# A hybrid trunk step on one core: first loads in order of need, and the first projection chunk with its parts outermost

## The chip, the cores and the metric

The kernel runs on one core of a Trainium2 chip. The metric is the device time of one execution in microseconds (us). The engines are TensorE (PE), VectorE (DVE), ScalarE (ACT) and GpSimd (POOL); SyncE (SP) only issues DMAs here.

## What is computed

One layer of a hybrid diffusion trunk over 384 tokens: 128 context tokens and 256 latent ones. The part that the change touches is its beginning:

```python
ada = silu(c) @ w_ada + b_ada                       # (1024) @ (1024, 6 * 1024), for context and for latents
sh1, sc1, g1, sh2, sc2, g2 = split(ada, 6)
n = rmsnorm(h, norm1_g) * (1 + sc1) + sh1           # h: 384 tokens x 1024
z = n @ w_in                                        # split into 14 parts: v, ic, q, k, u, ...
```

Behind it come neighbourhood attention, a gated convolution, a two-way gated scan (HGRN2), their mix through w_out, and a mixture of 64 experts with a shared one. All is fp32.

## The kernel before

All engines walk one list, `SCHEDULE`, built by `schedule()` (L161). A stage of it is issued by each engine that has a part in it, in the list's order, and semaphores join them; each engine works strictly in that order. An event `("unit", n)` is one group of products with one PSUM bank, `n % 2`. PE makes unit n only when unit n - 2 has been copied out by ACT.

Units 0 to 3 are adaLN: silu(c) times a piece of 512 columns of w_ada (L1534), eight products of 32 x 512 each, so that four pieces give shift and scale of the first norm. The units behind them are projections. The chunks "v" and "ic" are 512 columns of w_in each, with tokens on the partitions: three units of eight products (over k, the eight parts of D = 1024) by way of `product` (L1504). An fp32 product leaves two records in the trace, so a unit has 16.

Weights come through a ring of three slots of 2 MB in bigA. SP issues the loads in the order of `STREAM`: four pieces of w_ada, then "v", "ic", "q", "k" and so on. The load number n waits until the slot's earlier owner, n - 3, has been used. So w_ada's fourth piece waits for the first unit. x (1.5 MB) and the constants K (1.1 MB: identity, masks and so on) stand behind the third and fourth load in SP's order, and the two caches of 256 KB go on ACT's queue. POOL waits for the constants and then loads and masks attention's bias tiles.

The stage "norm1" stands after unit 1: ACT squares the three token tiles (L670), DVE makes the inverse root and the scaled tiles XN (L1088). The stage "mod1" stands after unit 3. PE first turns the 2048 modulation values into columns by 16 products with two moving columns (L1584, 32 records); each reads every eighth column of ADA. Then it transposes XN part by part (L1592), 24 transposes into banks 2 to 5. DVE forms the columns (L1056 to L1059) and writes the modulated nT from PSUM, two instructions for each part k (L1043, L1046). The first unit of "v" starts when all eight parts are written:

```python
if c == 0:
    pe.wait_ge(n_ready, KD)
```

Behind "v" ACT copies its units to V and rounds nT for the split products of "q" and the others; "ic" follows on PE directly. The split chunks, attention, the scan, the gates and the experts follow in the same list.

Of the kernel before, what the change touches and what calls it, by code (L numbers as in the profile page):

```python
# [21 lines left out]
P = 128  # L22
D = 1024
KD = D // P
NT = 3
# [27 lines left out]
K_ID, K_MASK, K_LEV, K_SCAN, K_SEL, K_TRI, K_ONE, K_R128, K_TOK, K_COL, K_T8, K_END, K_SUB = range(13)  # L53
K_W = [P, GRID_W, 7 * P, T, 2 * P, P, P, P, NT * 4, 2, NG * NG, 0, RTAB]
# [7 lines left out]
def shape_constants():  # L62
# [33 lines left out]
STREAM = ([("ada", n) for n in range(4)]  # L96
          + [x for n, name in enumerate(IN_CHUNKS)
             for x in [("in", n)] + ([("ada", ADA_IN[name])] if name in ADA_IN else [])]
# [14 lines left out]
def projection_units():  # L113

    units = []
    for n in range(4):
        units.append(("ada", n, 0))
# [96 lines left out]
def trunk(nc, x, consts, cols, b_gate, w_ada, w_in, w_br, w_out, rpb, cache_k, cache_v, state, w_router, b_router,  # L214
# [4 lines left out]
    with ExitStack() as ctx:  # L219
# [45 lines left out]
        ADA = bigB[:, 6144:8192]  # L265
        pair = sel[:, :, 0]
# [115 lines left out]
        xnt_ready = sem("normed_transposed")  # L382
        n_ready = sem("modulated")
# [3 lines left out]
        csil_zero = sem("csilu_padding_zeroed")  # L387
# [33 lines left out]
        at_zero = sem("pairwise_terms_zeroed")  # L421
# [76 lines left out]
        y_back = [sem(f"parts_loaded_{m}") for m in range(4 * NT)]  # L498
# [10 lines left out]
        def slot(key):  # L509
            return ring[:, SLOT_OF[key] % NSLOT, :]  # L510

# [31 lines left out]
        def _(sp):  # L543
# [106 lines left out]
        def _(act):  # L650
# [7 lines left out]
            act.dma_start(CK, cache_k).then_inc(in_cache, 16)  # L658
            act.dma_start(CV, cache_v).then_inc(in_cache, 16)
            for ev in SCHEDULE:  # L660
                st = ev[0]
                if st == "csilu":
                    act.wait_ge(in_cols, 16)
                    act.wait_ge(csil_zero, 1)
# [1285 lines left out]
```

## Time and profile before

| what | us |
|---|---|
| median of three runs | 1268.3 |
| lowest and highest run | 1262.52, 1287.38 |
| profiled execution, its time | 1289.7 |
| profiled execution, its span | 1287.9 |
| PE busy in it | 1162.2 |
| DVE, ACT, POOL busy in it | 446.9, 287.9, 180.8 |

The span runs from the first to the last instruction of one profiled execution. The profile page gives totals; the rows further down come from queries of the same trace: timelines by engine, lists of waits, DMA issues, and sums over stretches of time. In a timeline the first number is the start, the second the length, and the bracket holds the idle time ahead and what ended it. The granted clock is that of PE as a share of its full speed; the two levels are 1.2 and 2.4 GHz.

### The profile page before, as it was taken

Reading aid. Unit: us, or ns where it says so; the run is one execution under the profiler, and the core shown is the slowest. Engines: PE = TensorE matmul, PEld = TensorE weight load, DVE = VectorE, ACT = ScalarE, POOL = GpSimd, SP = SyncE. Lnnn points to the kernel's source line nnn. Section 1 sums busy time; section 2 is a strip of 40 time slices with the busy share of each in tenths; the row PEclk is TensorE's granted clock in tenths of the full one; section 3 lists DMA queues with packets and bytes.
Section 4 is the critical chain, followed back from the end, with each engine's and each line's share of the span. In section 5 each row is a group of like instructions: output and inputs, shape, how many; then the busy total and the mean of one; then the engine's idle time right before and its main releaser. Section 6 shows DMA issues by size and latency. Waiting matters only on the chain.

```text
span 1287.9 us, 14753 instructions
## 1 busy us (share of the span) xinstructions
PE 1162.2 (90%) x4912; PEld 713.0 (55%) x4912; DVE 446.9 (35%) x945; ACT 287.9 (22%) x429; POOL 180.8 (14%) x163
## 2 busy tenths in 40 slices
PE   2899988899988887799987999999999999999965
PEld 0549877678777765556454444444444444444422
DVE  0313333442787964333353121121221212212116
ACT  1022433334533432300121111111111111111101
POOL 0200222100332300000000411111111111111100
PEclk9799988889989998798987989999999999999978
DMA  9813555437444332140033869999999999999464
GB/s 355 219 65 131 95 81 79 74 132 274 160 151 153 125 139 82 53 142 17 1 131 157 319 259 386 401 390 377 378 393 387 376 386 407 392 392 391 178 275 181
DMA packets 85971, 292.40 MB, mean 227 GB/s; under 512 B 10330, under 2 KB 14554, under 8 KB 70682
## 3 DMA queue, kind: packets, MB, share of 16 engines
q1 hardware_dynamic: 69408, 259.10, 52.0%
q0 software_dynamic: 12976, 27.29, 9.2%
q10 hardware_dynamic: 3540, 5.39, 1.3%
q8 instruction: 29, 0.48, 0.2%
q14 instruction: 18, 0.15, 0.0%
HBM read 284.79 MB, written 25.30 MB: 241 GB/s over the span
## 4 chain that ended last, share of the span: by engine, by line
PE 55%; DVE 5%; DMA 2%; ACT 1%; issue 1%; DVEq 0%; SPq 0%; POOLq 0%
PE PS L1829 15%; PE PS L1504 12%; PE PS L1846 7%; PE PS L1831 7%; PE PS L1848 4%; PE PS L1815 3%; PE PS L1514 2%; PE PS L1896 1%; DMA bigA<-in_w_sh_down 1%; PE PS L1864 1%; PE PS L1695 1%; PE PS L1702 0%; DMA bigA<-y_parts 0%; PE PS L1676 0%; DVE bigC L1482 0%
## 5 line engine op out<-in xcount | busy, mean ns | idle before, releaser
L1552 PE MATMUL PS<-bigB_r 128*128 128x384 f32 x288 | 99.3, 345 | 3.3 <-ACT bigD L724 1.3
L1829 PE MATMUL PS<-bigB 128*128 128x512 f32 x224 | 101.7, 598 | 0.0
L964 POOL DMA_INDIRECT bigB<-n_rows,IDX x29 | 30.0, 1033 | 493.4 <-DVE IDX L1037 252.1
L1829 PE MATMUL PS<-bigA,bigB 128*128 128x512 f32 x208 | 97.9, 615 | 0.0
L1554 PE MATMUL PS<-bigB_r,bigA_r 128*128 128x384 f32 x288 | 97.5, 339 | 0.0
L1553 PE MATMUL PS<-nT_r,bigB_r 128*128 128x384 f32 x288 | 97.5, 338 | 0.0
L1832 PE MATMUL PS<-bigB 128*64 128x512 f32 x208 | 94.8, 599 | 0.0
L1831 PE MATMUL PS<-bigA,bigB 128*64 128x512 f32 x208 | 94.8, 599 | 0.0
L1461 DVE TENSOR_SCALAR bigB<-PS,bigD 128x1024 f32<-128x1024 f32 x40 | 51.4, 1284 | 104.8 <-PE PS L1846 70.6
L1103 DVE TENSOR_TENSOR bigA_r<-bigA,bigB_r 128x2048 fp32r<-128x2048 f32 x18 | 41.3, 2292 | 128.5 <-ACT bigB_r L746 128.5
L888 ACT ACTIVATE bigB<-PS 128x1024 f32<-128x1024 f32 x40 | 40.9, 1023 | 153.1 <-PE PS L1815 153.1
L1440 DVE TENSOR_TENSOR bigB<-bigB,PS 128x256 f32<-128x256 f32 x40 | 16.9, 421 | 162.4 <-ACT bigB L892 162.4
L1504 PE MATMUL PS<-bigA,nT 128*128 128x512 f32 x144 | 69.4, 645 | 4.2 <-DVE nT L1046 2.4
L1829 PEld LDWEIGHTS PS<-bigB 128*128 128x128 f32 x224 | 40.6, 191 | 41.1 <-issue 41.1
L724 ACT ACTIVATE bigB<-PS 128x384 f32<-128x384 f32 (+1 forms) x55 | 27.1, 495 | 159.0 <-PE PS L1554 66.0
L1552 PEld LDWEIGHTS PS<-bigB_r 128*128 128x128 f32 x288 | 55.1, 191 | 9.9 <-ACT bigD L724 3.3
L1829 PEld LDWEIGHTS PS<-bigA,bigB 128*128 128x128 f32 x208 | 38.6, 196 | 39.2 <-issue 38.9
L1036 DVE COPY bigD<-PS 128x1 f32<-128x1 f32 x44 | 7.0, 159 | 141.6 <-PE PS L1514 141.6
L1553 PEld LDWEIGHTS PS<-nT_r,bigB_r 128*128 128x128 f32 x288 | 55.1, 191 | 0.0
L1554 PEld LDWEIGHTS PS<-bigB_r,bigA_r 128*128 128x128 f32 x288 | 54.9, 191 | 0.0
L1504 PE MATMUL PS<-bigA,bigB 128*128 128x512 f32 x120 | 52.8, 595 | 1.6 <-ACT bigB L882 1.6
L1504 PEld LDWEIGHTS PS<-bigA,nT 128*128 128x128 f32 x144 | 29.5, 208 | 41.3 <-issue 39.2
(330 smaller groups left out, 2007.4 us busy)
## 6 DMA issues: line engine op xcount, KB each, us to landing
bigA<-in_w_in SPq DMA_DIRECT2D x17, 2048.0 KB, 8.7
bigB<-in_w_gate SPq DMA_DIRECT2D x27, 1024.0 KB, 8.5
bigB<-in_w_up SPq DMA_DIRECT2D x27, 1024.0 KB, 11.8
bigB<-in_w_down SPq DMA_DIRECT2D x27, 1024.0 KB, 12.0
bigA<-in_w_gate SPq DMA_DIRECT2D x26, 1024.0 KB, 6.7
bigA<-in_w_up SPq DMA_DIRECT2D x26, 1024.0 KB, 9.3
bigA<-in_w_down SPq DMA_DIRECT2D x26, 1024.0 KB, 12.9
bigA<-in_w_ada SPq DMA_DIRECT2D x12, 2048.0 KB, 10.4
```

Of the source, the lines that this page charges most:

```text
L888: nc.scalar.activation(XT[:, b, :, :].rearrange("p (a k) t -> p a (k t)", a=2), PS[:, 0:2, :], ACT.Copy).then_inc(xt_done, 1)
L1103: nc.vector.tensor_tensor(low, w, WHI[:, i % 2, :, :].bitcast(F32), ALU.subtract).then_inc(wlo_done, 1)
L1461: nc.vector.tensor_scalar(YS[:, p % 2, :].rearrange("p (a n) -> p a n", a=2), PS[:, 6:8, :], WC[:, p:p + 1], None, ALU.mult).then_inc(ys_d ...
L1504: last = mm(out, lhs(k), rhs(k), start=(k == 0), stop=(k == n - 1))
L1552: mm(out, wh, nh, start=(k == 0), stop=False)
L1553: mm(out, wh, nl, start=False, stop=False)
L1554: last = mm(out, wl, nh, start=False, stop=(k == KD - 1))
L1829: last = mm(PS[:, 2 + b, :], XT[:, b, k, :], GU_W[s][:, :, k, :], start=first, stop=stop)
L1831: mm(PS[0:HALF, 2 + b, :], XT[:, b, k, 0:HALF], GU_W[2][:, :, k, :], start=first, stop=stop)
L1832: last = mm(PS[HALF:P, 2 + b, :], XT[:, b, k, HALF:P], GU_W[3][:, :, k, :], start=first, stop=stop)
L1846: last = mm(PS[:, 6 + hf, :], HT[:, b, k, :], DN_W[s][:, k, cols], start=(k == 0), stop=(k == 1))
L1848: mm(PS[0:HALF, 6 + hf, :], HT[:, b, k, 0:HALF], DN_W[2][:, k, cols], start=(k == 0), stop=(k == 1))
```

## The change

The four early pieces of w_ada get homes of their own (`EARLY_W`, in bigB and bigD, whose later contents come after), and leave the ring. The ring begins with "v". The first loads are now issued without any wait: the vectors, the first 448 columns of the constants (identity, selector, window mask), w_ada 0 and 1, "v", w_ada 2 and 3, "ic", "q", then the rest of the constants and the two caches. x goes on ACT's queue. The wait counts of the semaphores that are used twice (`y_back`, `zeroed`, `modt_ready`, `mod_ready`, `in_x`) are raised to fit.

The columns of w_ada for the first shift and scale are stored in another order on the host, so that pieces 0 and 1 hold shift and scale of the parts k = 0 to 3 and pieces 2 and 3 those of k = 4 to 7, each part's 128 columns side by side.

The opening of the schedule is written out: norm1, unit 0, transposes of parts 0 to 3 ("xt", 0), modt 0, unit 1, xt 1, modt 1, mods 0; then the steps vk 0 to vk 7, with units 2 and 3 behind vk 1 and vk 2, and modt 2, modt 3 and mods 1 behind vk 3. A step vk makes the three products of one part k, one for each token tile, each with a bank of its own (4, 5, 6), so that "v" accumulates over the steps. A modt is four of the former sixteen products. ACT copies the transposed tokens from PSUM to nT, and DVE modulates them there in place, part by part, once the half's columns are formed.

```diff
@@ -50,8 +50,8 @@
 TAIL_BANK = (0, 2, 6)
 
 
-K_ID, K_MASK, K_LEV, K_SCAN, K_SEL, K_TRI, K_ONE, K_R128, K_TOK, K_COL, K_T8, K_END, K_SUB = range(13)
-K_W = [P, GRID_W, 7 * P, T, 2 * P, P, P, P, NT * 4, 2, NG * NG, 0, RTAB]
+K_ID, K_SEL, K_MASK, K_LEV, K_SCAN, K_TRI, K_ONE, K_R128, K_TOK, K_COL, K_T8, K_END, K_SUB = range(13)
+K_W = [P, 2 * P, GRID_W, 7 * P, T, P, P, P, NT * 4, 2, NG * NG, 0, RTAB]
...
+EARLY = 4
+
+
+STREAM = ([x for n, name in enumerate(IN_CHUNKS)
+           for x in [("in", n)] + ([("ada", ADA_IN[name])] if name in ADA_IN else [])]
...
-    s = [("csilu",)]
+    s = [("csilu",), ("norm1",), ("unit", 0), ("xt", 0), ("modt", 0), ("unit", 1), ("xt", 1), ("modt", 1), ("mods", 0)]
+    for k in range(KD):
+        s.append(("vk", k))
+        if k in (1, 2):
+            s.append(("unit", k + 1))
+        if k == 3:
+            s += [("modt", 2), ("modt", 3), ("mods", 1)]
     att = 0
     fill = []
     for n, (name, c, j) in enumerate(UNITS):
+        if n < EARLY:
+            continue
...
-        if n == 1:
-            s.append(("norm1",))
-        if n + 1 == AFTER[("ada", 3)]:
-            s.append(("mod1",))
...
+        EARLY_W = [bigB[:, 9216:13312], bigB[:, 13312:17408], bigB[:, 17408:21504], bigD[:, 0:4096]]
...
+        early_ada = y_back[0:EARLY]
...
+        def bank_of(n):
+            return 4 + UNITS[n][2] if UNITS[n][0] == "v" else n % 2
...
+            sp.dma_start(K[:, 0:K_AT[K_LEV]], consts[:, 0:K_AT[K_LEV]]).then_inc(in_x, 16)
             for n in ISSUE:
                 src, i = STREAM[n]
+                if n < 2:
+                    for c in (2 * n, 2 * n + 1):
+                        sp.dma_start(EARLY_W[c].rearrange("p (k n) -> p k n", k=KD),
+                                     wa[:, :, c * WCH:(c + 1) * WCH]).then_inc(early_ada[c], 16)
                 if n == NSLOT:
-                    sp.dma_start(X, x.rearrange("(m p) d -> p m d", p=P)).then_inc(in_x, 16)
-                if n == NSLOT + 1:
-                    sp.dma_start(K[:], consts[:, 0:K_AT[K_END]]).then_inc(in_small, 16)
+                    sp.dma_start(K[:, K_AT[K_LEV]:K_AT[K_END]], consts[:, K_AT[K_LEV]:K_AT[K_END]]).then_inc(in_small, 16)
+                    sp.dma_start(CK, cache_k).then_inc(in_cache, 16)
+                    sp.dma_start(CV, cache_v).then_inc(in_cache, 16)
...
-            act.dma_start(CK, cache_k).then_inc(in_cache, 16)
-            act.dma_start(CV, cache_v).then_inc(in_cache, 16)
+            act.dma_start(X, x.rearrange("(m p) d -> p m d", p=P)).then_inc(in_x, 16)
...
-                    act.wait_ge(in_x, 16)
+                    act.wait_ge(in_x, 32)
...
+                elif st == "xt":
+                    for k in range(4 * ev[1], 4 * ev[1] + 4):
+                        act.wait_ge(xnt_ready, k + 1)
+                        nc.scalar.activation(nT[:, k, :], PS[:, 2 + k % 4, 0:T], ACT.Copy).then_inc(xt_copied, 1)
...
+            pool.wait_ge(in_x, 32)
...
-            def modulate(which, ready, done):
-
-                for k in range(KD):
-                    dve.wait_ge(ready, k + 1)
-                    nc.vector.tensor_scalar(nT[:, k, 0:CTX], PS[:, 2 + k % 4, 0:CTX], modc[:, which + 1, 0, k:k + 1],
-                                            modc[:, which, 0, k:k + 1], ALU.mult, ALU.add).then_inc(dve_order, 1)
-                    chain[0] += 1
-                    nc.vector.tensor_scalar(nT[:, k, CTX:T], PS[:, 2 + k % 4, CTX:T], modc[:, which + 1, 1, k:k + 1],
-                                            modc[:, which, 1, k:k + 1], ALU.mult, ALU.add).then_inc(done, 1)
-                dve.wait_ge(done, KD)
-                dve.wait_ge(dve_order, chain[0])
-
-            def mod_columns(which, bank, nvec, norm, cnt):
-
-                src = PS[:, bank, 0:32].rearrange("p (s k v) -> p s v k", s=2, v=2)
+            def modulate(k0):
+
+                for k in range(k0, k0 + 4):
+                    dve.wait_ge(xt_copied, k + 1)
+                    for v, toks in enumerate((slice(0, CTX), slice(CTX, T))):
+                        ins = nc.vector.tensor_scalar(nT[:, k, toks], nT[:, k, toks], modc[:, 1, v, k:k + 1],
+                                                      modc[:, 0, v, k:k + 1], ALU.mult, ALU.add)
+                        if v == 0:
+                            ins.then_inc(dve_order, 1)
+                            chain[0] += 1
+                        else:
+                            ins.then_inc(n_ready, 1)
+                if k0 > 0:
+                    dve.wait_ge(n_ready, KD)
+                    dve.wait_ge(dve_order, chain[0])
...
-                elif st == "mod1":
+                elif st == "mods":
+                    hf = ev[1]
                     dve.wait_ge(in_cols, 16)
-                    dve.wait_ge(modt_ready, 1)
-                    mod_columns(0, 7, 2, cc(C_N1), 1)
-                    modulate(0, xnt_ready, n_ready)
+                    dve.wait_ge(modt_ready, hf + 1)
+                    mod_columns(0, slice(4 * hf, 4 * hf + 4), cc(C_N1), hf + 1)
+                    modulate(4 * hf)
...
+                    if name == "v":
+                        continue
                     if n >= 2:
-                        pe.wait_ge(unit_taken, n - 1)
-                    bank = n % 2
+                        pe.wait_ge(unit_taken, EARLY if n in (AFTER["v"], AFTER["v"] + 1) else n - 1)
+                    bank = bank_of(n)
                     if name == "ada":
                         if c == 0:
                             pe.wait_ge(csil_ready, 1)
-                        arrived(pe, ("ada", c))
-                        w = slot(("ada", c)).rearrange("p (k n) -> p k n", k=KD)
+                        if c < EARLY:
+                            pe.wait_ge(early_ada[c], 16)
+                        else:
+                            arrived(pe, ("ada", c))
+                        w = (EARLY_W[c] if c < EARLY else slot(("ada", c))).rearrange("p (k n) -> p k n", k=KD)
...
-                elif st == "mod1":
-
-                    pe.wait_ge(unit_taken, 4)
-                    pe.wait_ge(in_small, 16)
-                    for s in range(2):
-                        for k in range(KD):
-                            last = mm(PS[:, 7, (s * KD + k) * 2:(s * KD + k) * 2 + 2], ADA[:, s * D + k:(s + 1) * D:KD],
-                                      pair, start=True, stop=True)
-                    last.then_inc(modt_ready, 1)
-                    pe.wait_ge(xn_ready, NT)
-                    for k in range(KD):
+                elif st == "modt":
+
+                    c = ev[1]
+                    hf, s_ = c // 2, c % 2
+                    pe.wait_ge(unit_taken, c + 1)
+                    pe.wait_ge(in_x, 32)
+                    for k in range(4 * hf, 4 * hf + 4):
+                        at = c * WCH + k % 4 * P
+                        last = mm(PS[:, 7, (s_ * KD + k) * 2:(s_ * KD + k) * 2 + 2], ADA[:, at:at + P], pair, start=True, stop=True)
+                    if s_ == 1:
+                        last.then_inc(modt_ready, 1)
+                elif st == "vk":
+
+                    k = ev[1]
+                    if k == 0:
+                        arrived(pe, ("in", 0))
+                        pe.wait_ge(xt_copied, KD)
+                    pe.wait_ge(n_ready, k + 1)
+                    w = slot(("in", 0)).rearrange("p (k n) -> p k n", k=KD)
+                    for j in range(NT):
+                        ins = mm(PS[:, bank_of(EARLY + j), :], nT[:, k, j * P:(j + 1) * P], w[:, k, :], start=(k == 0), stop=(k == KD - 1))
+                        if k == KD - 1:
+                            ins.then_inc(unit_ready, 1)
+                elif st == "xt":
+                    if ev[1] == 0:
+                        pe.wait_ge(xn_ready, NT)
+                    for k in range(4 * ev[1], 4 * ev[1] + 4):
                         if k >= 4:
-                            pe.wait_ge(n_ready, k - 3)
+                            pe.wait_ge(xt_copied, k - 3)
                         for m in range(NT):
                             last = nc.tensor.transpose(PS[:, 2 + k % 4, m * P:(m + 1) * P], XN[:, m, k:D:KD], ident)
                         last.then_inc(xnt_ready, 1)
...
+    first = w_ada[:, 0:2 * D].reshape(D, 2, P, 2, 4).transpose(0, 3, 1, 4, 2).reshape(D, 2 * D)
+    w_ada = np.concatenate([first, w_ada[:, 2 * D:]], 1)
```

## Rows read from the trace of the kernel before

**Rows 1.** The page's head: span, and busy time of PE.

```profile
span 1287.9 us, 14753 instructions
...
PE 1162.2 (90%) x4912; PEld 713.0 (55%) x4912; DVE 446.9 (35%) x945; ACT 287.9 (22%) x429; POOL 180.8 (14%) x163
```

**Rows 2.** Timeline of PE, 0 to 75 us: start, length, instructions, idle time before.

```profile
14.06 3.64 PE L1534 MATMUL PS<-bigA,csil 128*32 128x512 f32 x16 [14.06 <-DMA bigA<-in_w_ada]
19.39 3.64 PE L1534 MATMUL PS<-bigA,csil 128*32 128x512 f32 x16 [1.68 <-DMA bigA<-in_w_ada]
24.89 1.92 PE L1534 MATMUL PS<-bigA,csil 128*32 128x512 f32 x16 [1.86 <-DMA bigA<-in_w_ada]
34.13 3.23 PE L1534 MATMUL PS<-bigA,csil 128*32 128x512 f32 x16 [7.32 <-DMA bigA<-in_w_ada]
38.08 7.80 PE L1584 MATMUL PS<-K,bigB 128*128 128x2 f32 x32 [0.71 <-ACT bigB L691]
45.73 5.12 PE L1592 MATMUL PS<-K,bigB 128*128 128x128 f32 x24
53.22 22.11 PE L1504 MATMUL PS<-bigA,nT 128*128 128x512 f32 x47 [2.36 <-DVE nT L1046]
```

**Rows 3.** Waits of PE over the whole execution: us in total, times, longest.

```profile
PE PS L1534 <- DMA bigA<-in_w_ada: 24.9, 4, 14.1
```

**Rows 4.** Timeline of ACT, 0 to 75 us; same columns.

```profile
28.64 1.06 ACT L670 ACTIVATE bigB<-bigB 128x1024 f32<-128x1024 f32 x1 [4.95 <-DMA bigB<-in_x]
...
62.06 0.60 ACT L724 ACTIVATE bigB<-PS 128x512 f32<-128x512 f32 x1 [24.03 <-PE PS L1504]
68.92 0.60 ACT L724 ACTIVATE bigB<-PS 128x512 f32<-128x512 f32 x1 [6.27 <-PE PS L1504]
```

**Rows 5.** Timeline of SP's queue, 55 to 200 us.

```profile
75.78 83.99 SPq L564 DMA_DIRECT2D bigA<-in_w_in  x5
```

**Rows 6.** DMA around the first issues: issues and landings, ACT's queue, packets; x by its line.

```profile
bigA<-in_w_ada SPq DMA_DIRECT2D x1, 2048.0 KB, 12.8
...
bigC<-in_cache_v ACTq DMA_DIRECT2D x1, 256.0 KB, 3.4
...
DMA packets 1206, 2.30 MB, mean 338 GB/s; under 512 B 93, under 2 KB 93, under 8 KB 1206
q10 hardware_dynamic: 276, 0.50, 20.1%
...
DMA to landing us min/median/max: 20.2/20.2/20.2
```

**Rows 7.** DMA packets moved from 0 to 14 us and from 0 to 17.5 us.

```profile
DMA packets 2216, 4.19 MB, mean 299 GB/s; under 512 B 192, under 2 KB 192, under 8 KB 2216
...
DMA packets 2901, 5.56 MB, mean 318 GB/s; under 512 B 207, under 2 KB 207, under 8 KB 2901
```

**Rows 8.** Timeline of DVE, 0 to 75 us; columns as in group 2.

```profile
34.49 2.08 DVE L1088 TENSOR_SCALAR bigB<-bigB,small 128x1024 f32<-128x1024 f32 x3
45.98 0.38 DVE L1056 TENSOR_TENSOR modc<-PS,C 128x16 f32<-128x16 f32 x2 [9.41 <-PE PS L1584]
...
47.15 0.53 DVE L1046 TENSOR_SCALAR nT<-PS,modc 128x256 f32<-128x256 f32 x1
```

**Rows 9.** Stretches of the opening: busy time of each engine, granted clock, DMA share, GB/s.

```profile
45.00:50.00 5.00, 5.00 (x24) 5.00 (x25) 3.88 (x13) 0.00 (x0) 0.00 (x0) 0.50 0.77 209
...
54.00:55.00 1.00, 1.00 (x2) 0.34 (x1) 0.00 (x0) 0.00 (x0) 0.00 (x0) 0.50 1.16 145
...
58.00:59.00 1.00, 1.00 (x4) 0.52 (x3) 0.00 (x0) 0.00 (x0) 0.00 (x0) 1.00 0.47 41
```

**Rows 10.** Timeline of POOL, before 75 us and from 100 to 150 us.

```profile
60.15 1.41 POOL L950 TENSOR_TENSOR bigC<-bigC,K 128x256 f32<-128x256 f32 x2 [6.24 <-DMA bigC<-in_rpb]
...
139.69 2.52 POOL L945 DMA_DIRECT2D bigC<-in_rpb  x4 [78.14 <-DVE bigC L1121]
```

**Rows 11.** Weight loads of L1504, 0 to 100 us: min, median, max in ns.

```profile
L1504 PEld LDWEIGHTS PS<-bigA,nT x96: 186/190/338, 53.2 to 95.3; 128*128 128x128 f32 x96
```

More of the change, by code:

```diff
@@ L94 @@
 ADA_PLACE = {c: n for n, c in enumerate((4, 5, 10, 11, 6, 7, 8, 9))}
-STREAM = ([("ada", n) for n in range(4)]
-          + [x for n, name in enumerate(IN_CHUNKS)
-             for x in [("in", n)] + ([("ada", ADA_IN[name])] if name in ADA_IN else [])]
+EARLY = 4
+STREAM = ([x for n, name in enumerate(IN_CHUNKS)
+           for x in [("in", n)] + ([("ada", ADA_IN[name])] if name in ADA_IN else [])]
           + [("br", n) for n in range(3)]
@@ L115, in projection_units @@
     units = []
-    for n in range(4):
+    for n in range(EARLY):
         units.append(("ada", n, 0))
@@ L382, in trunk @@
         xnt_ready = sem("normed_transposed")
+        xt_copied = sem("normed_transposed_copied")
         n_ready = sem("modulated")
@@ L420, in trunk @@
         lev_taken = sem("level_taken")
[L421 removed]
+        zeroed = sem("csilu_padding_then_pairwise_terms_zeroed")
         kh_done = sem("carry_keys")
@@ L497, in trunk @@
         scat = sem("results_added")
-        y_back = [sem(f"parts_loaded_{m}") for m in range(4 * NT)]
+        y_back = [sem(f"early_ada_then_parts_loaded_{m}") for m in range(4 * NT)]
+        early_ada = y_back[0:EARLY]
         part_ready = sem("parts_summed")
@@ L676, in _ @@
                     name, c, j = UNITS[n]
-                    ps = PS[:, n % 2, :]
+                    ps = PS[:, bank_of(n), :]
                     act.wait_ge(unit_ready, n + 1)
@@ L953, in _ @@
             pool.wait_ge(conv_done, 4)
-            nc.gpsimd.memset(AT_, 0.0).then_inc(at_zero, 1)
+            nc.gpsimd.memset(AT_, 0.0).then_inc(zeroed, 1)
             for n in SPLIT_G:
@@ L1054, in mod_columns @@
+            def mod_columns(which, ks, norm, cnt):
+                n = ks.stop - ks.start
+                src = PS[:, 7, 0:32].rearrange("p (s k v) -> p s v k", s=2, v=2)
                 b = cc(C_ADA).rearrange("p (s k) -> p s k", s=4)
                 for s in range(2):
-                    link(nc.vector.tensor_tensor(modc[:, which + s, :, :], src[:, s, :, :],
-                                                 b[:, which + s, :].unsqueeze(1).broadcast_to([P, 2, KD]), ALU.add))
-                link(nc.vector.tensor_scalar(modc[:, which + 1, :, :], modc[:, which + 1, :, :], 1.0, None, ALU.add))
@@ L1059, in mod_columns @@
-                nc.vector.tensor_tensor(modc[:, which + 1, :, :], modc[:, which + 1, :, :],
-                                        norm.unsqueeze(1).broadcast_to([P, 2, KD]), ALU.mult).then_inc(mod_ready, 1)
+                    link(nc.vector.tensor_tensor(modc[:, which + s, :, ks], src[:, s, :, ks],
+                                                 b[:, which + s, ks].unsqueeze(1).broadcast_to([P, 2, n]), ALU.add))
+                link(nc.vector.tensor_scalar(modc[:, which + 1, :, ks], modc[:, which + 1, :, ks], 1.0, None, ALU.add))
@@ L1061, in mod_columns @@
+                nc.vector.tensor_tensor(modc[:, which + 1, :, ks], modc[:, which + 1, :, ks],
+                                        norm[:, ks].unsqueeze(1).broadcast_to([P, 2, n]), ALU.mult).then_inc(mod_ready, 1)
                 dve.wait_ge(mod_ready, cnt)
@@ L1066, in take_level @@
                 if i == 0:
-                    dve.wait_ge(at_zero, 1)
+                    dve.wait_ge(zeroed, 2)
                 if i > 0:
@@ L1299, in _ @@
                 elif st == "mod2":
-                    dve.wait_ge(modt_ready, 2)
-                    mod_columns(2, 7, 2, cc(C_N2), 2)
+                    dve.wait_ge(modt_ready, 3)
+                    mod_columns(2, slice(0, KD), cc(C_N2), 3)
                 elif st == "gate1":
@@ L1479, in residual @@
                 link(nc.vector.tensor_tensor(XH[:, m, :], XH[:, m, :], YSUM[:, 0, :], ALU.add))
-                dve.wait_ge(y_back[4 * m + 3], 16)
+                dve.wait_ge(y_back[4 * m + 3], 32 if m == 0 else 16)
                 link(nc.vector.tensor_tensor(YSUM[:, 1, :], last[:, 0, :], last[:, 1, :], ALU.add))
@@ L1723, in _ @@
                     pe.wait_ge(mix_done, 2 * KD)
-                    pe.wait_ge(mod_ready, 2)
+                    pe.wait_ge(mod_ready, 3)
                     arrived(pe, ("out", hf))
@@ L1892, in _ @@
                 for c in range(3):
-                    pe.wait_ge(y_back[4 * m + c], 16)
+                    pe.wait_ge(y_back[4 * m + c], 32 if 4 * m + c < EARLY else 16)
                     for r in range(2):
```

9 lines of the change are left out of this document (3 added, 6 removed).

## Prediction

> **What bounds the kernel now.** I read the page's totals first [rows 1]: TensorE (PE) is busy for 1162.2 of 1287.9 us. One engine carries nearly the whole kernel, so what counts is how early its long uninterrupted run begins. The timeline of PE over the opening [rows 2] shows where that is: four short bursts of adaLN products (L1534), each with a gap ahead of it, then 7.80 us of transposes of the modulation vector (L1584), 5.12 us of transposes of the normed tokens (L1592), a gap of 2.36 us, and from 53.22 us on the projection products of L1504 without a break. The list of PE's waits [rows 3] puts a number on the gaps: 24.9 us in four waits for pieces of w_ada, 14.1 of them before anything could start, and 2.4 us for the modulated tokens. The timeline of ScalarE (ACT) marks the ends of the products of "v": its first two units are copied out at 62.06 and 68.92 us [rows 4]. The SP queue, which may load "k" once "v" is through, issues at 75.78 us [rows 5]. So "v" ends and "ic" starts at 75.8 us, and this is the point that I follow: everything behind it is the same work in the same order.
>
> **The loads.** Before, w_ada's first piece is issued at 1.2 us and lands 12.8 us later, at 14.0 us [rows 6]. By then 4.19 MB had moved [rows 7], though only 2.67 MB stand in front of it and in it (44 KB of vectors, twice 256 KB of caches, 2048 KB). A piece therefore lands about 1.5 MB after its place in the order. In the new order the first piece has 0.05 + 0.23 (the first 448 columns of the constants) + 1.57 (x) + 2.10 = 3.95 MB up to its own end. With the same 1.5 MB it lands when 5.45 MB have moved, at about 17.4 us [rows 7]. That is 3.4 us later than now. If it needed no such surplus it would land at 13.5 us (4.19 MB moved by 14). The bursts of L1534 start 5.3 and 5.5 us apart [rows 2], which is one piece of 2 MB; so after it come w_ada 1 at 22.8, w_in for "v" at 28.2, w_ada 2 at 33.6, w_ada 3 at 39.0 and "ic" at 44.4 us.
>
> x goes on ACT's queue beside it. The caches there moved 0.50 MB by 9 us and the second landed 3.4 us after its issue, while w_ada's first needed 12.8 [rows 6]: the two queues share, and the smaller load is not put behind the larger. At half of some 340 GB/s x lands near 11 us. The norm takes 7.9 us from its first square at 28.64 [rows 4] to the end of the scaled tiles at 36.57 us [rows 8]. XN is then ready at 19 us, under the first adaLN unit, and costs nothing; for each microsecond that x lands after 13, everything moves by one.
> The Trainium skill (DMA: Bandwidth & Descriptors, section Queues, rings and completion order) says that each DMA engine takes turns between the queues that have work, a packet of descriptors at a time. The row of the caches agrees. x's runs are of 4 KB and w_ada's of 2 KB, so by that rule x would have about two thirds of the bandwidth and land near 9 us, with no change to the sum.
>
> **The steps on PE.** Units take 3.64 us at the lower clock and 1.92 us at the higher; both stand in the same list [rows 2]. 24 transposes take 5.12 us, so a group of 12 takes 2.6; the 32 records of L1584 take 7.80 us, so a modt of eight takes 1.95.
> - From 17.4 us: unit 0 3.64, xt 0 2.6, modt 0 1.95, unit 1 3.64, xt 1 2.6, modt 1 1.95. That ends at 33.8 us. I take the lower clock for both units, since the stretch of transposes ran at 0.50 of the clock [rows 9]. The higher clock for the second would save 1.7. ACT's copies of a unit, 0.6 each, lie under the transposes.
> - The vector engine's (DVE) columns and its first modulated slice: 45.98 to 46.82 for the columns, and the first slice's second part starts at 47.15 and takes 0.53 [rows 8]. With the 0.25 us from PE's end to DVE's start that is 1.9 us on the path. The first k step starts at 35.7 us. "v" landed long before (28.2).
> - A k step is three products, six records. A unit of 16 records took 6.86 us from copy to copy (62.06 to 68.92), so a step takes 2.58 us at full clock. Four steps are 10.3 us, and units 2 and 3 between them 2 x 1.92 = 3.8. Their data (33.6 and 39.0 us) is there when they come, at about 43 and 48 us. PE's first unit of "v" took 8.84 us instead of 6.86, because the granted clock was 0.50 early in it and 1.00 only later [rows 9]. I charge the same 1.9 here. This part ends at 51.7 us.
> - modt 2 and modt 3, 3.9 us, to 55.6. Nothing else is left in PE's order here, so DVE's 1.9 us is bare again, to 57.5.
> - k steps 4 to 7: 10.3 us, and since PE has just idled and done only small products, another 1.9 for the clock. "v" ends at 69.7 us. DVE's later slices need 0.8 each, under 2.58.
>
> The gain at this point is 75.8 - 69.7 = 6.1 us. In words: about 20 us of waiting between units vanish, but the first piece comes 3.4 us later, x and both halves' small steps now stand in PE's order one behind another, and 1.9 us of DVE and of clock are paid twice. What limits the opening is no longer the loads but PE's own small steps.
>
> The smaller edits cost nothing. ACT's eight extra copies out of PSUM (a 128x512 copy takes 0.60 [rows 4]) run ahead of the modulation while PE transposes. The three copies of "v" come together, but "ic" has two free banks and needs 6.86 us for each unit. The rest of the constants and the caches are now behind "q", at about 52 to 54 us instead of 37, and with them the bias tiles of attention: the second head's tile, masked by 61.6 us before, then stands near 77 us, while the load of the third, which the first head's scores free, goes only at 139.69 us [rows 10]. "k" is issued as "v" ends in both kernels. modt now reads w_ada's columns side by side, not every eighth; the pace could fall from 0.244 to the 0.19 us that a contiguous weight load took [rows 11], worth up to 1.7 us over the four. I take none of it.
>
> **Does it reach the end?** PE has work from there on; its later waits are for DVE and ACT, which move along with it, and the loads of the expert stage are issued as PE frees slots. I take all of it. The profiled execution of 1287.9 us would become 1281.8. It lies 19.6 us over the median of the runs, 1268.3, so the forecast is 1268.3 - 6.1 = 1262 us.
>
> **Rivals.**
> - A, more is won. Unit 1 at the higher clock (1.7), the first piece landing early so that only XN at 19 us holds the second step (2.1), contiguous weight loads (1.7), no clock loss (3.8): together 9.3 more, 1253 us. For it: each alone has a row. Against: it needs several at once.
> - B, the other side: the granted clock stays at half through the first four k steps. The rows of 45 to 50 us show 0.50 with PE fully busy on small products [rows 9], and the new order mixes small products with large ones. The 14.1 us of steps and units would then take 28.2, 12.2 more than charged, "v" ends at 81.9 and the time is 1274 us. It turns slower than before once PE spends over 16 us of this chunk at half clock. Against it: one unbroken stretch of such products was back at 1.00 by 58 us, 5 us after it began [rows 9].
> - C, x lands late: were it served in turn behind both first pieces, it would need the 20.2 us that it needs now [rows 6], XN would be ready near 29 us instead of 21 at the latest, and the time is 8 us worse: 1270 us, no change.
> - D, the gain is spent later: a wait for a load or a bias that stands still in time while PE moves. I found none that is close (some 60 us of slack for the bias). 1268 us.
>
> **Chances.** Forecast (2 to 10 us won) 0.58, A 0.17, B 0.10, C 0.05, D 0.10. The cases span 1253 to 1274 us, and the three runs of the kernel before already span 25 us, so a median can sit some microseconds off. The range is 1250 to 1276 us. Two per cent, about what a measurement of this kernel can tell from no change, is 25 us, more than any case gives alone. Faster by over 2% takes A and a low set of runs: 0.09. Slower by over 2% takes B and a high one: 0.04. The rest, 0.87, is within 2%.
>
> **What would show it.** In the profile after: the first L1534 burst at about 17.4 us; the first k step at 35.7; no wait for w_ada above 1 us after unit 0; the last modt near 55.6 and a gap of about 1.9 us behind it; "k" issued at 69.7 instead of 75.8; the granted clock back at 1.00 within some 5 us of the first k step. A first burst near 14 us or no 0.50 behind 35 us speaks for A, a 0.50 that lasts to unit 3 for B, a square later than 13 us for C, a new wait behind 75 us for D.

## The result, and the profile after

| | before | after |
|---|---|---|
| median of the runs of this comparison, us | 1274.28 (4) | 1259.34 (4) |
| lowest and highest, us | 1262.52, 1287.38 | 1250.99, 1262.51 |
| ratio to before, with its 95% interval | | 0.9863 [0.9815, 0.9912] |
| span of the profiled execution, us | 1287.9 | 1260.7 |
| end of "v" in it, us | 75.78 | 58.05 |

The kernel is faster by 1.4%, some 17 us by the ratio and 15 us between the medians. The forecast was 1262 us, so the time itself came out within 3 us, but that is luck. Its gain of 6.1 us did not come out: the gain at the end of "v" is 17.7 us, nearly three times as large, and above rival A's 15.4. The level agreed because the median that the forecast started from, 1268.3 us of three runs, lies 6 us under the median with a fourth run. The measured ratio on that starting point would have been 1251 us, just inside the range. The profiled execution of the kernel before (1289.7 us) was a slow one, so its whole span says little; "v" and what stands ahead of it are compared by their own times.

The timeline of PE in the changed kernel, 0 to 80 us (start, length, instructions, idle time before and its releaser), to be laid beside [rows 2]:

```profile
13.43 3.33 PE L1565 MATMUL PS<-bigB,csil 128*32 128x512 f32 x16 [13.43 <-DMA bigB<-in_w_ada]
16.69 1.60 PE L1637 MATMUL PS<-K,bigB 128*128 128x128 f32 x12
18.13 0.95 PE L1615 MATMUL PS<-K,bigB 128*128 128x2 f32 x8
19.02 1.92 PE L1565 MATMUL PS<-bigB,csil 128*32 128x512 f32 x16
20.87 1.61 PE L1637 MATMUL PS<-K,bigB 128*128 128x128 f32 x12
22.32 0.95 PE L1615 MATMUL PS<-K,bigB 128*128 128x2 f32 x8
25.00 5.39 PE L1627 MATMUL PS<-bigA,nT 128*128 128x512 f32 x12 [1.73 <-DVE nT L1064]
30.32 1.92 PE L1565 MATMUL PS<-bigB,csil 128*32 128x512 f32 x16
32.17 2.84 PE L1627 MATMUL PS<-bigA,nT 128*128 128x512 f32 x6
36.51 1.92 PE L1565 MATMUL PS<-bigD,csil 128*32 128x512 f32 x16 [1.49 <-DMA bigD<-in_w_ada]
38.36 2.84 PE L1627 MATMUL PS<-bigA,nT 128*128 128x512 f32 x6
41.04 1.84 PE L1615 MATMUL PS<-K,bigB 128*128 128x2 f32 x16
44.52 13.50 PE L1627 MATMUL PS<-bigA,nT 128*128 128x512 f32 x24 [1.64 <-DVE nT L1064]
57.85 20.76 PE L1530 MATMUL PS<-bigA,nT 128*128 128x512 f32 x48
```

From 13.43 us to the end of "v" PE stands still three times, for 4.9 us in all. L1627 is a k step, L1615 a modt, L1637 the transposes, L1530 the products of "ic". The list of PE's waits says the same; the 24.9 us for w_ada in [rows 3] have become 14.9:

```profile
PE PS L1565 <- DMA bigB<-in_w_ada: 13.4, 1, 13.4
...
PE PS L1627 <- DVE nT L1064: 3.4, 2, 1.7
...
PE PS L1565 <- DMA bigD<-in_w_ada: 1.5, 1, 1.5
```

x landed 7.1 us after its issue at 0.73, and ACT's first square started at 8.09 us instead of 28.64 [rows 4]. It waited for x and for the first constants, and the constants came last. The list of DMA issues and ACT's timeline:

```profile
bigB<-in_x ACTq DMA_DIRECT2D x1, 1536.0 KB, 7.1
```
```profile
8.09 1.06 ACT L685 ACTIVATE bigB<-bigB 128x1024 f32<-128x1024 f32 x1 [4.36 <-DMA K<-in_consts]
```

And SP issues "k" as "v" ends, which answers [rows 5]:

```profile
58.05 21.14 SPq L580 DMA_DIRECT2D bigA<-in_w_in  x2
```

### The profile page after: what moved, and what is told of

Same layout as the page of the kernel before. It is cut to its first block, busy times and chain, and to the rows that moved or that the text cites. A ratio compares the mean times of both kernels' runs of the same rounds, so it can differ in the third digit from the quotient of the medians.

```text
span 1260.7 us, 14771 instructions
## 1 busy us (share of the span) xinstructions
PE 1144.5 (91%) x4912; PEld 700.2 (56%) x4912; DVE 446.7 (35%) x949; ACT 291.3 (23%) x437; POOL 180.6 (14%) x163
## 4 chain that ended last, share of the span: by engine, by line
PE 53%; DVE 4%; DMA 4%; ACT 1%; issue 1%; DVEq 0%; SPq 0%; POOL 0%; POOLq 0%
PE PS L1874 14%; PE PS L1530 12%; PE PS L1891 7%; PE PS L1876 7%; PE PS L1893 3%; PE PS L1860 3%; DMA y_parts<-bigB,IDX 2%; PE PS L1540 2%; PE PS L1941 1%; DMA bigA<-in_w_sh_down 1%; DMA nT<-n_rows,IDX 1%; PE PS L1909 1%; PE PS L1740 1%; PE PS L1747 0%; DMA bigA<-y_parts 0%
## 5 line engine op out<-in xcount | busy, mean ns | idle before, releaser
L1874 PE MATMUL PS<-bigA,bigB 128*128 128x512 f32 x208 | 94.9, 599 | 0.0
L1530 PE MATMUL PS<-bigA,bigB 128*128 128x512 f32 x120 | 52.8, 595 | 1.6 <-ACT bigB L901 1.6
L1231 DVE TENSOR_TENSOR bigB<-bigB 128x384 f32<-128x384 f32 x56 | 52.4, 996 | 0.4
L1876 PEld LDWEIGHTS PS<-bigA,bigB 128*64 128x64 f32 x208 | 26.3, 136 | 46.3 <-issue 44.5
## 6 DMA issues: line engine op xcount, KB each, us to landing
bigB<-in_w_gate SPq DMA_DIRECT2D x27, 1024.0 KB, 10.5
```

The source lines that it names most:

```text
L1231: ins = nc.vector.tensor_tensor(cutb(E[:, d, :])[:, :, s], a, c, ALU.subtract)
L1530: last = mm(out, lhs(k), rhs(k), start=(k == 0), stop=(k == n - 1))
L1874: last = mm(PS[:, 2 + b, :], XT[:, b, k, :], GU_W[s][:, :, k, :], start=first, stop=stop)
L1876: mm(PS[0:HALF, 2 + b, :], XT[:, b, k, 0:HALF], GU_W[2][:, :, k, :], start=first, stop=stop)
```

## The experiments

The end of "v" in the profiled execution is the measure for the opening: one execution for each kernel. The ratio of the times to the kernel before, on the same chip, is the measure for the whole.

| kernel | first piece used | end of "v" | span less that | ratio of times, 95% |
|---|---|---|---|---|
| before | 14.06 | 75.78 | 1212.1 | 1 |
| before_again | 11.97 | 74.35 | 1209.1 | |
| columns_alone | 10.46 | 69.50 | 1202.3 | 0.9958 [0.9925, 0.9991] |
| old_order | 11.37 | 82.01 | 1201.9 | 1.0095 [1.0056, 1.0133] |
| v_behind_ada | 13.72 | 66.65 | 1194.7 | 0.9952 [0.9910, 0.9994] |
| strided_columns | 13.38 | 62.36 | 1202.6 | 0.9895 [0.9843, 0.9947] |
| all_units_first | 13.75 | 59.98 | 1198.2 | 0.9932 [0.9889, 0.9974] |
| changed | 13.43 | 58.05 | 1202.7 | 0.9863 [0.9815, 0.9912] |
| changed_again | 13.39 | 55.52 | 1202.5 | 0.9867 [0.9824, 0.9910] |
| x_on_sp | 13.88 | 56.01 | 1202.3 | 0.9846 [0.9788, 0.9904] |
| filled_gap | 13.40 | 55.18 | 1205.4 | 0.9865 [0.9783, 0.9947] |
| cover | 13.68 | 52.19 | 1201.6 | 0.9896 [0.9828, 0.9964] |
| cover_again | 13.65 | 52.84 | 1203.2 | 0.9820 [0.9779, 0.9862] |

### Both kernels again

> The kernel before, unchanged, once more. It asks how much of the 27.2 us between the two profiled spans is the change. At the end of 'v' the two profiles differ by 17.7 us (75.78 against 58.05); the identical work behind that point took 1212.1 us in the profile before and 1202.7 in the one after. Theory 'phases' (the 9.5 us behind are granted-clock luck of one execution): the opening repeats to within 1 us ('v' ends at 75 to 76.5), while the work behind it takes another value anywhere from 1190 to 1215 us, low where the mean granted clock is high. Theory 'carried' (the change also speeds up what follows): it again takes 1210 us or more.

> The changed kernel, unchanged, beside the others of this group on one chip. Theory 'the shift at the end of v is the gain': 'v' ends 16 to 18 us before it does in the kernel before (74.4 and 75.8 there), and the time is shorter by the same 16 to 18 us, a ratio of 0.986 to 0.988. Theory 'part of it is spent later': the ratio is 0.990 or more, that is under 13 us.

The opening of before repeats, only its first piece lands 2 us earlier, and "v" ends 0.65 us ahead of the stretch that I gave. PE's timeline:

```profile
11.97 3.63 PE L1534 MATMUL PS<-bigA,csil 128*32 128x512 f32 x16 [11.97 <-DMA bigA<-in_w_ada]
...
36.64 7.80 PE L1584 MATMUL PS<-K,bigB 128*128 128x2 f32 x32 [0.71 <-ACT bigB L691]
44.30 5.36 PE L1592 MATMUL PS<-K,bigB 128*128 128x128 f32 x24
51.78 43.13 PE L1504 MATMUL PS<-bigA,nT 128*128 128x512 f32 x96 [2.12 <-DVE nT L1046]
```

The repeat of the changed kernel ended "v" at 55.52 us, 18.8 and 20.3 us ahead and so more than I had expected, while its ratio lies in the expected 0.986 to 0.988. The pairs differ by 16.3 to 20.3 us at the end of "v", and the two ratios of 0.9863 and 0.9867 are 17 us each (0.0133 x 1278.9 = 17.0). So the shift is about all of the gain, and it is carried to the end; the intervals of the ratios, some 6 us either way, leave room for a few microseconds more or less. The work behind took 1209.1 us in this repeat, which alone would not exclude that some gain arises there. columns_alone speaks against it: behind "v" it is the kernel before, and it took 1202.3 us, as the changed kernel does. So do the times: the median of before beside changed_again, 1278.9 us, less 1.8 (the difference of time and span) and some 75 us up to the end of "v", leaves 1202 as well. The 9.5 us by which the two first profiles differ further are a matter of the single execution.

### The layout of w_ada's columns

```diff
-    first = w_ada[:, 0:2 * D].reshape(D, 2, P, 2, 4).transpose(0, 3, 1, 4, 2).reshape(D, 2 * D)
+    first = w_ada[:, 0:2 * D].reshape(D, 2, P, 2, 4).transpose(0, 3, 1, 2, 4).reshape(D, 2 * D)
...
-                        last = mm(..., ADA[:, at:at + P], pair, start=True, stop=True)
+                        last = mm(..., ADA[:, c * WCH + k % 4:(c + 1) * WCH:4], pair, start=True, stop=True)
```

> The changed kernel, but each part's 128 columns of shift and scale lie four apart in ADA instead of side by side (they lay eight apart before the change); all else is the same. Theory 'layout': the weight loads of the modt products take about 300 ns as before the change (336) and not 190, eight records take 1.7 to 1.95 us instead of 0.95, and 'v' ends 3 to 4 us later, at 61 to 62 us. Theory 'clock': the halving of the modt products came from the granted clock alone; loads stay at 190 ns, eight records at 0.95, and 'v' ends at 58 us.

PE's timeline and the weight loads of the line (min, median, max in ns):

```profile
18.48 1.92 PE L1614 MATMUL PS<-K,bigB 128*128 128x2 f32 x8
...
43.45 3.67 PE L1614 MATMUL PS<-K,bigB 128*128 128x2 f32 x16
```
```profile
L1614 PEld LDWEIGHTS PS<-K,bigB x32: 307/329/329, 18.4 to 46.7; 128*128 128x128 f32 x32
```

Layout it is: 1.92 us for eight records against 0.95 (line L1615 above), 3.67 for sixteen against 1.84, with the granted clock at 1.00 in both kernels. Three such pieces on the path are 0.97 + 0.97 + 1.83 = 3.8 us. "v" ended 4.3 and 6.8 us later than in the two executions of the changed kernel; here the clock also fell at the first k steps, which took 7.08 us instead of 5.39. The converse, the kernel before with this part alone:

```diff
-                            last = mm(..., ADA[:, s * D + k:(s + 1) * D:KD],
+                            last = mm(..., ADA[:, s * D + k * P:s * D + (k + 1) * P],
...
+    first = w_ada[:, 0:2 * D].reshape(D, 2, P, KD).transpose(0, 1, 3, 2).reshape(D, 2 * D)
+    w_ada = np.concatenate([first, w_ada[:, 2 * D:]], 1)
```

> The kernel before with one part of the change alone: w_ada's first 2048 columns are stored on the host so that the 128 columns of each part lie side by side, and L1584 reads them so. Loads, ring and schedule are those of before. Theory 'layout': weight loads of L1584 take 190 ns instead of 336, its 32 records take about 3.8 us instead of 7.80, and 'v' ends 4 us earlier, at 70.3 to 71.8 us against 74.35 and 75.78; the time is 4 us shorter, a ratio of 0.996 to 0.998. Theory 'clock': at half clock, as in the kernel before, the loads are bound by the clock and not by the stride; the records stay above 0.2 us apart and 'v' ends less than 1.5 us earlier.

```profile
34.88 4.70 PE L1584 MATMUL PS<-K,bigB 128*128 128x2 f32 x32 [0.71 <-ACT bigB L691]
```
```profile
L1584 PEld LDWEIGHTS PS<-K,bigB x32: 186/192/337, 34.9 to 39.2; 128*128 128x128 f32 x32
```

4.70 us instead of 7.80, 3.1 us of the 4.9 to 6.3 by which "v" ends earlier; the rest is a first piece that landed earlier. I had expected 3.8 us for the 32 records. They took longer because the clock fell while PE made them (stretches of this kernel, columns as in [rows 9]):

```profile
36.00:37.00 1.00, 1.00 (x11) 1.00 (x11) 0.00 (x0) 0.00 (x0) 0.48 (x1) 1.00 1.03 383
37.00:38.00 1.00, 1.00 (x9) 1.00 (x8) 0.00 (x0) 0.00 (x0) 0.00 (x0) 0.71 1.06 391
38.00:39.00 1.00, 1.00 (x6) 1.00 (x7) 0.00 (x0) 0.00 (x0) 0.00 (x0) 0.50 1.24 305
```

A single contiguous load took 192 ns up to 37 us and 333 ns behind 38 us. With the stride of eight it was 334 to 338 ns at either level of the clock (kernel before, 38.8 to 44.9 us, granted 1.00 up to 40). So the layout shortens a load at full clock only, and theory "clock" had a part as well.

The ratio of 0.9958 is 5.4 us, with an interval of 1.1 to 9.6. A column order on the host and the line that reads it give some fifth of the whole gain.

### The order of the loads

```diff
-            act.dma_start(X, ...).then_inc(in_x, 16)
+            act.dma_start(CK, cache_k).then_inc(in_cache, 16)
+            act.dma_start(CV, cache_v).then_inc(in_cache, 16)
...
-            sp.dma_start(K[:, 0:K_AT[K_LEV]], ...).then_inc(in_x, 16)
...
+                if n == 0:
+                    for c in range(EARLY):
+                        if c == 3:
+                            sp.dma_start(X, ...).then_inc(in_x, 16)
+                        sp.dma_start(EARLY_W[c]..., wa[:, :, c * WCH:(c + 1) * WCH]).then_inc(early_ada[c], 16)
+                    sp.dma_start(K[:, 0:K_AT[K_LEV]], ...).then_inc(in_x, 16)
+                    sp.dma_start(K[:, K_AT[K_LEV]:K_AT[K_END]], ...).then_inc(in_small, 16)
```

> The changed kernel with the loads issued in the order of before: the vectors, w_ada 0 to 2, x, w_ada 3, all constants, 'v', 'ic', 'q', the caches on ACT's queue; the homes outside the ring stay, so nothing waits for a slot. Theory 'order': XN is ready only near 36 us, after x at 28, and the constants (identity) at 37, so the first transposes start at 37 us, the first k step not before 'v' lands at 42 to 43, and 'v' ends at 68 to 72 us: most of the gain is gone. Theory 'homes': what mattered was that no load waits for a unit; 'v' ends at 60 to 64 us.

"Order" was right in kind and short in size: "v" ends at 82.0 us, 10 later than I gave, and the kernel is slower than before (1.0095). The timelines of ACT and of PE:

```profile
31.90 1.06 ACT L685 ACTIVATE bigB<-bigB 128x1024 f32<-128x1024 f32 x1 [28.30 <-DMA K<-in_consts]
```
```profile
39.88 2.82 PE L1637 MATMUL PS<-K,bigB 128*128 128x128 f32 x12 [24.88 <-DVE bigB L1113]
```

The new schedule puts norm1 and the transposes ahead of unit 1, so with the old order PE stands 24.9 us before units that it could have made. And the squares wait for the first constants too, which I had not counted. The new order on PE without the new order of the loads is worse than the kernel before, and homes outside the ring do not help it. The converse, the new loads under the old schedule, was not tried, so how the gain divides between loads and schedule stays open.

```diff
-                if n < 2:
-                    for c in (2 * n, 2 * n + 1):
+                if n == 0:
+                    for c in range(EARLY):
```

> The changed kernel with one edit in SP's order: the weights of 'v' are loaded behind the fourth piece of w_ada and not between the second and third. Theory 'the place of v decides': all four steps that could run early now wait, the first k step starts when 'v' lands, at 36 to 37 us instead of 25.0, and 'v' ends at 59 us or later, 1 to 4 us behind. Theory 'only the sum of bytes decides': by 36.5 us everything has landed in either order, the small steps are all done by then, nothing interrupts the k steps but one modt, and 'v' ends at 57 to 58 us, the same time.

The place of "v" decides, as the first theory says, but by far more than its 1 to 4 us: "v" ends 8.6 to 11.1 us behind the changed kernel. The ratio of 0.9952 leaves 6 of the 17 us. PE's timeline:

```profile
35.32 8.16 PE L1627 MATMUL PS<-bigA,nT 128*128 128x512 f32 x12 [11.56 <-DMA bigA<-in_w_in]
43.41 1.92 PE L1565 MATMUL PS<-bigB,csil 128*32 128x512 f32 x16
...
52.57 1.84 PE L1615 MATMUL PS<-K,bigB 128*128 128x2 f32 x16
```

Units 2 and 3 stand behind k steps 1 and 2 in PE's order. Their data had landed (w_ada 3 at 29.8 us), but they could not run while step 0 waited 11.56 us for "v". The granted clock fell to 0.50 in this wait, and the first steps then took 8.16 us instead of 5.39. "v" ended at 66.65 us.

x on SP's queue instead of ACT's:

```diff
-            act.dma_start(X, x.rearrange("(m p) d -> p m d", p=P)).then_inc(in_x, 16)
...
+            sp.dma_start(X, x.rearrange("(m p) d -> p m d", p=P)).then_inc(in_x, 16)
```

> The changed kernel with x issued on SP's queue, behind the first constants and ahead of w_ada 0, instead of on ACT's; the bytes ahead of each piece are the same. Theory 'one pool of bytes': x lands at 7 to 9 us (7.8 on ACT's queue), the first piece at 13.3 to 14.3 and the fourth at 35 to 37, 'v' ends within 1.5 us of the changed kernel's 55.5 to 58.1, the time is the same. Theory 'two queues start faster': everything lands 1.5 us or more later and 'v' ends at 58 to 60 us.

As the first theory says. ACT's first square came at 8.34 us (8.09 on its own queue), the first piece at 13.88, "v" ended at 56.01. The queue is worth nothing here; what old_order lost came with the place in the order.

### Four steps ahead of the second half

```diff
-    for k in range(KD):
-        s.append(("vk", k))
-        if k in (1, 2):
-            s.append(("unit", k + 1))
-        if k == 3:
-            s += [("modt", 2), ("modt", 3), ("mods", 1)]
+    s += [("unit", 2), ("unit", 3), ("modt", 2), ("modt", 3), ("mods", 1)]
+    s += [("vk", k) for k in range(KD)]
...
+                    if c == 2:
+                        pe.wait_ge(mod_ready, 1)
```

> The new loads are kept, but no k step stands ahead of the second half of w_ada: all four adaLN units and modts first, then the eight k steps in one stretch. Theory 'steps matter': w_ada 3 still lands at 36.5 us, so unit 3 1.9, copy and modt 3 1.5, columns 1.6, and only then 24 products of 20.6: 'v' ends at 62.5 to 64 us instead of 58.05, the time is 4 to 6 us longer than that of the changed kernel. Theory 'loads are all': the clock stays up through one unbroken stretch where it now falls to half for 6.8 us, so 'v' ends within 2 us of 58.05 and the time is that of the changed kernel.

```profile
30.01 3.64 PE L1561 MATMUL PS<-bigB,csil 128*32 128x512 f32 x16 [6.09 <-DMA bigB<-in_w_ada]
35.44 1.92 PE L1561 MATMUL PS<-bigD,csil 128*32 128x512 f32 x16 [1.79 <-DMA bigD<-in_w_ada]
37.29 1.95 PE L1613 MATMUL PS<-K,bigB 128*128 128x2 f32 x16
39.10 20.85 PE L1625 MATMUL PS<-bigA,nT 128*128 128x512 f32 x48
```

"v" ended at 59.98 us, just within the 2 us of "loads are all" by the first profile of the changed kernel and outside them by the second. The first steps need only the first half's columns, so there was no wait for DVE behind modt 3 and no fall of the clock: 24 products in 20.85 us. The early steps save 1.9 to 4.5 us at the end of "v" (59.98 against 58.05 and 55.52). The ratio of 0.9932 lies 0.0065 over that of changed_again, 8 us, with intervals that overlap and from another group of runs. So the steps ahead are a small part of the gain.

### The gap behind modt 3

```diff
     for k in range(KD):
+        if k == 3:
+            s += [("modt", 2), ("modt", 3), ("mods", 1)]
         s.append(("vk", k))
         if k in (1, 2):
             s.append(("unit", k + 1))
-        if k == 3:
-            s += [("modt", 2), ("modt", 3), ("mods", 1)]
```

> The changed kernel with modt 2, modt 3 and mods 1 moved ahead of k step 3, so that this step's 2.6 us run while DVE forms the second half's columns. The bare wait of 1.64 us at 42.9 goes. Theory 'the gap lets the clock fall': with no gap the granted clock stays at 1.00 from 44 to 50 us as well, 'v' ends at 53 to 54.5 us, 4 to 5 us earlier. Theory 'the small products let it fall': the clock still goes to half for some 7 us, and 'v' ends at 56 to 57 us, 1 to 2 us earlier.

> The variant with modt 2, modt 3 and mods 1 ahead of k step 3 once more, now beside the changed kernel. In its first profile 'v' ended at 52.19 instead of 58.05 with the granted clock at 1.00 throughout. Theory 'the gap lets the clock fall' expects that to repeat (51.5 to 53) and 4 to 7 us less than the changed kernel in time. Theory 'luck of the windows': the clock falls in this execution, 'v' ends at 55 to 57, and the two are within 3 us.

Stretches of the changed kernel (columns as in [rows 9]) and of this one, with PE's timeline of cover:

```profile
44.00:46.00 2.00, 1.48 (x2) 0.84 (x3) 2.00 (x8) 0.00 (x0) 0.00 (x0) 0.50 1.08 415
46.00:48.00 2.00, 2.00 (x3) 0.67 (x2) 0.20 (x1) 0.00 (x0) 0.00 (x0) 0.50 0.98 392
48.00:50.00 2.00, 2.00 (x4) 0.87 (x3) 0.00 (x0) 0.00 (x0) 0.00 (x0) 0.50 0.34 127
```
```profile
44.00:46.00 2.00, 2.00 (x7) 0.80 (x6) 0.00 (x0) 0.00 (x0) 0.00 (x0) 1.00 1.09 423
46.00:48.00 2.00, 2.00 (x6) 0.94 (x5) 0.00 (x0) 0.00 (x0) 0.00 (x0) 1.00 0.96 384
```
```profile
37.23 1.95 PE L1615 MATMUL PS<-K,bigB 128*128 128x2 f32 x16
39.04 13.12 PE L1627 MATMUL PS<-bigA,nT 128*128 128x512 f32 x30
```

In both executions of cover the clock stayed at 1.00 and "v" ended at 52.2 and 52.8 us, 2.7 to 5.9 before the changed kernel's. Five steps take 13.12 us, four took 13.50 and 12.26 in the changed kernel. To tell the gap from the small products ahead of it, two products that nobody reads fill it:

```diff
                     if s_ == 1:
                         last.then_inc(modt_ready, 1)
+                    if c == 3:
+                        w = slot(("in", 0)).rearrange("p (k n) -> p k n", k=KD)
+                        for i in range(2):
+                            mm(PS[:, 2, :], nT[:, i, 0:P], w[:, i, :], start=(i == 0), stop=(i == 1))
```

> The changed kernel with two extra products of 512 columns behind modt 3, whose result nobody reads (1.7 us at full clock), so that PE doesn't idle while DVE forms the second half's columns. Theory 'the gap lets the clock fall': the granted clock stays at 1.00 up to the end of 'v', the last 24 products take 10.4 us instead of 12.3 to 13.5, and though PE does more work 'v' ends 1.9 to 3.1 us earlier than it did with the gap (55.5 and 58.05, of which 1.5 was a wait for w_ada 3): 53.5 to 55.5 us. Theory 'the small products let it fall': the clock still drops to half behind modt 2 and 3, the last products take 12 us or more, and 'v' ends at 55.5 us or later.

PE's timeline, and the stretch:

```profile
36.57 1.92 PE L1565 MATMUL PS<-bigD,csil 128*32 128x512 f32 x16 [1.58 <-DMA bigD<-in_w_ada]
...
42.80 1.96 PE L1621 MATMUL PS<-bigA,nT 128*128 128x512 f32 x4
```
```profile
44.00:46.00 2.00, 2.00 (x6) 0.70 (x5) 2.00 (x8) 0.00 (x0) 0.00 (x0) 1.00 1.06 406
```

This execution is level with the changed kernel's first profile up to modt 3, the wait of 1.5 us for w_ada 3 included. With the gap filled the clock stays at 1.00, and "v" ends 2.9 us earlier (55.18 against 58.05) though PE does more.

So closing the gap keeps the clock up: it stayed at 1.00 in all four executions that go from modt 3 to the k steps without a pause (all_units_first, cover, cover_again, filled_gap), and it fell to 0.50 in five of the six with the pause of 1.64 us. But the theories were put too simply, for the gap alone is not the cause. In v_behind_ada the same sixteen records stand ahead of the same pause, and the clock stayed at 1.00:

```profile
56.05 10.57 PE L1627 MATMUL PS<-bigA,nT 128*128 128x512 f32 x24 [1.64 <-DVE nT L1064]
```
```profile
56.00:58.00 2.00, 1.95 (x5) 1.00 (x6) 1.73 (x6) 0.00 (x0) 0.00 (x0) 1.00 0.81 39
```

Nor are small products harmless. The pause of 1.73 us behind modt 1 left the clock at 1.00 in the changed kernel, while in strided_columns, where modt 1 takes twice as long, it fell behind the same pause. And in columns_alone it fell with no pause at all, within 3 us of small products. What decides between these cases the runs do not show.

cover is the best version at the end of "v". The times do not show it: within one group of runs its ratio of 0.9820 stands against 0.9867 of the changed kernel, with intervals that overlap, but in another group it was 0.9896, above both ratios of the changed kernel. So the 2.7 to 5.9 us are shown by the profiles alone.

## Why the prediction was right or wrong, point by point

- **What bounds the opening.** Right: the gaps between units, then PE's own small steps. Between 13.43 us and the end of "v" PE is idle for 4.9 us only.
- **The landing of the first piece: 17.4 us forecast, 13.4 measured.** This was the first wrong term. I had taken from one execution that a piece lands 1.5 MB after its place in the order. In before_again it was 0.8 MB (3.45 MB moved by 11.97 us, 2.67 in the order), in the changed kernel 0.3 (4.26 moved by 13.4 us, 3.95 in the order). The packets up to that point, of before_again and of the changed kernel:

```profile
DMA packets 1855, 3.45 MB, mean 288 GB/s; under 512 B 192, under 2 KB 192, under 8 KB 1855
```
```profile
DMA packets 1882, 4.26 MB, mean 318 GB/s; under 512 B 192, under 2 KB 320, under 8 KB 1882
```

  The four executions with the old order used the piece at 10.5 to 14.1 us, the nine executions with the new one at 13.4 to 13.9. By the means of these two groups the new order costs some 1.6 us, not 3.4 (an estimate, from a spread of 3.6 us), and the surplus is not a constant. My own other case, 13.5 us without a surplus, was the measured value.
- **The small steps of the first half: 16.4 us forecast, 9.8 measured** (13.43 to 23.27). The second wrong term, and the largest. I charged the slower pace throughout, from rows of before in which PE had waited or the clock stood at 0.50. The new order runs these steps one behind another, and after the first unit they went at the faster pace: unit 1 took 1.92 instead of 3.64, twelve transposes 1.60 instead of 2.6, which no rival had priced. And modt fell from 1.95 to 0.95 by the layout, of which I took nothing and allowed 1.7 us over all four; it is worth 3.8. One reading under these prices was wrong: I called 3.64 us the price of a unit at the lower clock, but the granted clock was recorded as 1.00 under the first two units of before, as it is under unit 0 now (3.33 us). Both paces are in the rows, but here the recorded clock does not explain them (first unit of before):

```profile
15.00:16.00 1.00, 1.00 (x12) 0.35 (x8) 0.00 (x0) 0.00 (x0) 0.00 (x0) 1.00 1.05 397
```

- **The first k step: 1.9 us behind the modt forecast, 1.73 measured.**
- **Steps 0 to 3 with units 2 and 3: 16.0 us forecast, 16.0 measured** (25.00 to 41.04), but by other parts: no loss of clock (forecast 1.9), and 1.49 us for w_ada 3 instead. I had said that no data would be late; w_ada 3 even landed earlier than forecast (36.5 us against 39.0), but PE was there 13 us earlier (35.0 against 48). In changed_again it came without a wait, so this term is 0 to 1.5 us by the execution. That the sums agree is luck.
- **modt 2 and 3: 3.9 forecast, 1.84 measured. The bare wait behind them: 1.9 forecast, 1.64 measured.** The mechanism was right.
- **Steps 4 to 7: 12.2 us forecast, 13.5 measured**, by the mechanism given: the clock fell behind the gap, here for 6.6 us, which costs 1.3 more than charged; in changed_again it fell for 3.4 us, and the steps took 12.26.
- **Together:** 4.0 + 6.6 + 0.2 + 2.1 + 0.3 - 1.3 = 11.9 us earlier than the 69.7 forecast; measured 58.05, 11.65 earlier.
- **Does it reach the end:** right, as far as the intervals tell. Ratio and shift agree at some 17 us, so D did not happen.
- **Rivals.** A happened nearly whole: unit 1 at the higher clock, the early first piece, the contiguous loads, and no loss of clock at the first step; only the loss at steps 4 to 7 stayed. I had called it unlikely (0.17) because it needs several. They were perhaps not independent: the faster unit 1 and the first steps without a loss both go with a PE that hardly waits (1.73 us between 13.43 and 35 us), but no run separates them. A's 9.3 us fell short of the 11.65: the transposes (2.0) were not in it, the first piece had 2.1 of the 4.0 and the layout 1.7 of the 3.8, while the clock's share at steps 4 to 7 did not come. B did not happen: 25 to 43 us were at 1.00 (one stretch of the changed kernel below). C did not: x landed at 7.8 us.

```profile
26.00:28.00 2.00, 2.00 (x6) 0.88 (x5) 0.59 (x3) 0.00 (x0) 0.00 (x0) 1.00 1.05 388
```

The rule of the Trainium skill on queues that take turns (DMA: Bandwidth & Descriptors, Queues, rings and completion order) gave 9 us for x, and my estimate at half the bandwidth 11; it landed at 7.8, nearer the rule. But x_on_sp shows that nothing hung on it.

## What to carry to other kernels

A price taken from a stretch in which an engine keeps stopping need not be the price in a stretch in which it doesn't: when a change removes waits, cost PE's small steps at both paces that the rows show and ask which goes with the new order. A column order chosen on the host is worth trying by itself where a product is all weight load. And an engine's order must follow that of its loads: the new order on PE under the old loads was slower than either kernel.

## What the runs showed of the hardware

A weight load of 128 x 128 fp32 with its columns side by side took 192 ns in the median where the granted clock was 1.00 (the changed kernel's modts, columns_alone up to 37 us) and 333 ns where it was 0.50 (columns_alone from 38 us). With a stride of four it took 329 ns at 1.00 (strided_columns), with a stride of eight 334 to 338 ns at either level (the kernel before).

A pause of 1.64 us behind sixteen records of small products went with a fall of the granted clock to 0.50 in five executions (the changed kernel twice, x_on_sp, old_order, strided_columns) and not in a sixth (v_behind_ada). With the pause covered or filled, or the steps free of it, the clock stayed at 1.00 in all four executions. Without a pause it fell in columns_alone, within 3 us of products that are nearly all weight load.
